# The second stream of the RWKV mixer runs 37 of its 74 stages behind the first, on every engine

## The reference

```python
def step(s, inp):
    r_t, w_t, k_t, v_t, kk_t, a_t = inp
    sa = jnp.einsum('bhij,bhj->bhi', s, -kk_t)
    s = (s * w_t[:, :, None, :] + sa[..., None] * (kk_t * a_t)[:, :, None, :]
         + v_t[..., None] * k_t[:, :, None, :])
    return s, jnp.einsum('bhij,bhj->bhi', s, r_t)
...
y = ((y - mean) * lax.rsqrt(var + GN_EPS) * p['rwkv_ln_w'][j].reshape(H_B, N_B)
     + p['rwkv_ln_b'][j].reshape(H_B, N_B))
y = y + jnp.sum(r * kb * p['rwkv_r_k'][j], axis=-1, keepdims=True) * v
o_b = y.reshape(bsz, T, D_B) * gate
```

## Time and profile before

| | |
|---|---|
| median of three runs | 3694.82 us (3686.28 to 3708.57) |
| span of the profiled execution | 3677.0 us |
| PE busy | 3407.4 us, 93% |
| DVE, ACT, POOL busy | 46%, 32%, 45% |
| mean granted clock of TensorE | 0.947 |
| RWKV mixer within the span | about 603.0 to 921.5 us |

### The profile page before, as it was taken

The page is one execution under the profiler, slowest core; times in us unless marked ns, Lnnn a source line. Parts: engine busy times, 40 slices in busy tenths (PEclk is TensorE's granted clock), DMA queues, the critical chain, the costliest instruction groups (busy, mean ns, idle before and its releaser), DMA issues.

```text
span 3677.0 us, 63816 instructions
## 1 busy us (share of the span) xinstructions
PE 3407.4 (93%) x24784; PEld 3270.7 (89%) x24784; DVE 1678.0 (46%) x2251; ACT 1169.2 (32%) x1384; POOL 1643.6 (45%) x1038
## 2 busy tenths in 40 slices
PE   7998896857879999999999799998979999999997
PEld 7998885846879999999999699985979999999997
DVE  3236667485563332233334546814563332233345
ACT  3244443231333332233322235421233332233322
POOL 4556773000444444544444455721444445444443
PEclk9999997978889999999999899986989999999999
DMA  5443331000424444444443444542424444444442
GB/s 166 151 150 111 122 105 55 4 24 15 153 88 149 148 150 159 137 149 148 148 159 133 148 145 124 173 144 120 145 91 148 148 155 154 137 149 148 155 150 107
DMA packets 118658, 474.81 MB, mean 129 GB/s; under 512 B 13425, under 2 KB 15089, under 8 KB 115569
## 3 DMA queue, kind: packets, MB, share of 16 engines
q1 hardware_dynamic: 108864, 421.58, 35.8%
q10 hardware_dynamic: 9648, 51.17, 3.6%
HBM read 450.66 MB, written 22.03 MB: 129 GB/s over the span
## 4 chain that ended last, share of the span: by engine, by line
PE 86%; DVE 9%; ACT 2%; issue 1%; POOL 1%; DMA 1%; ACTq 0%; DVEq 0%; POOLq 0%
PE ps L316 50%; PE ps L320 25%; DVE M L462 1%; PE ps L1719 1%; PE ps L1739 1%; DVE xn L425 1%; PE ps L837 1%; PE ps L1316 1%; POOL x_lo L433 1%; PE ps L418 0%; PE ps L1318 0%; PE ps L1280 0%; DVE Z L718 0%; PE ps L1265 0%; PE ps L1482 0%
## 5 line engine op out<-in xcount | busy, mean ns | idle before, releaser
L291 POOL TENSOR_TENSOR w_lo<-raw,w_hi 128x512 fp32r<-128x512 f32 (+2 forms) x756 | 1463.6, 1937 | 1734.7 <-ACT w_hi L280 1733.9
L316 PE MATMUL ps<-x_hi,w_hi 128*128 128x320 f32 x5024 | 1515.7, 315 | 89.8 <-POOL x_lo L433 71.8
L316 PE MATMUL ps<-x_lo,w_hi 128*128 128x320 f32 x5024 | 1504.1, 313 | 0.0
L280 ACT ACTIVATE w_hi<-raw 128x1024 fp32r<-128x1024 f32 (+1 forms) x756 | 840.8, 1113 | 1654.3 <-PE ps L320 1618.2
L316 PEld LDWEIGHTS ps<-x_hi,w_hi 128*128 128x128 f32 x5024 | 959.8, 191 | 107.9 <-issue 73.6
L291 DVE TENSOR_TENSOR w_lo<-raw,w_hi 128x512 fp32r<-128x512 f32 (+1 forms) x640 | 515.8, 807 | 1030.0 <-ACT w_hi L280 1012.1
L316 PEld LDWEIGHTS ps<-x_lo,w_hi 128*128 128x128 f32 x5024 | 961.8, 191 | 0.6
L320 PE MATMUL ps<-x_hi,w_lo 128*128 128x320 f32 x5024 | 846.4, 311 | 1.9 <-POOL w_lo L291 1.9
L320 PEld LDWEIGHTS ps<-x_hi,w_lo 128*128 128x128 f32 x5024 | 769.5, 189 | 2.9 <-POOL w_lo L291 2.9
L316 PE MATMUL ps<-u_hi,w_hi 128*128 128x320 f32 x1408 | 415.5, 310 | 6.3 <-DVE u_lo L530 6.3
L316 PE MATMUL ps<-u_lo,w_hi 128*128 128x320 f32 x1408 | 415.1, 309 | 0.0
(11 more groups left out here) (359 smaller groups left out, 2606.9 us busy)
## 6 DMA issues: line engine op xcount, KB each, us to landing
raw<-in_w_ffn_in SPq DMA_DIRECT2D x352, 512.0 KB, 3.5
raw<-in_w_ffn_out SPq DMA_DIRECT2D x128, 704.0 KB, 4.0
raw<-in_w_in_even SPq DMA_DIRECT2D x116, 512.0 KB, 3.5
raw<-in_w_in_odd SPq DMA_DIRECT2D x96, 512.0 KB, 3.5
raw<-in_w_out_even SPq DMA_DIRECT2D x32, 512.0 KB, 3.5
raw<-in_w_out_odd SPq DMA_DIRECT2D x32, 512.0 KB, 3.5
hS<-in_state_hgrn ACTq DMA_DIRECT2D x4, 1024.0 KB, 5.5
out_hgrn_s<-hS ACTq DMA_DIRECT2D x4, 1024.0 KB, 4.9
```

What stands on the lines that cost most here:

```text
L280: nc.scalar.activation(w_hi[s % 2][:, 0:g.kt, :], raw[s % 4][:, 0:g.kt, :], ACT.Copy)\
L291: eng.tensor_tensor(w_lo[s % 2][:, k0:k1, :], raw[s % 4][:, k0:k1, :], w_hi[s % 2][:, k0:k1, :].bitcast(f32), sub).then_inc(sem(f"split_lo ...
L316: nc.tensor.matmul(out, w_hi[s % 2][:, k, :], x[:, kk, :], start=half == 0 and k == 0 and x is xh, stop=False)
```

## The change

Stream 1 gets the stage numbers of its groups raised by ROFF = 37. On every engine the instructions are the same ones as before; only how the two streams are merged changes. Stream 0 passes through its first 37 stages alone, stream 1 through its last 37 alone; between them one stream's stages 37 to 73 stand beside the other's stages 0 to 36, three times. Waits on semaphores, buffers and banks are unchanged.

```diff
-        RJ, RGROUPS, RSTAGES = 2, 4, 74
+        RJ, RGROUPS, RSTAGES, ROFF = 2, 4, 74, 37
...
# rwkv_act, rwkv_dve and rwkv_pe:
-                j0, at0 = RJ * g, G * RSTAGES
+                j0, at0 = RJ * g, G * RSTAGES + ROFF * x
...
# rwkv_pool:
-                yield G * RSTAGES + 6
+                yield G * RSTAGES + ROFF * x + 6
```

## The result

| | before | after |
|---|---|---|
| time, median | 3701.7 us (4 runs, 3686.3 to 3710.4) | 3770.8 us (4 runs, 3761.9 to 3776.7) |
| ratio | | 1.020, 95% interval 1.017 to 1.024 |
| span of the profiled execution | 3677.0 us | 3774.8 us |
| RWKV mixer in it (last L799 to L296) | 318.5 us | 393.3 us |

The change makes the kernel 2% slower, and the mixer accounts for it. VectorE does the same work. TensorE's busy time has grown by 66 us though its instructions are the same. ScalarE (ACT) has seven instructions more, 1391 for 1384: all of them are loads of an activation table, which the text of the kernel does not contain. In the mixer these loads went from 9 to 16, at 1.28 us each. Two streams in like stages shared one load for each kind of function; now almost every group needs its own. What they cost is told behind the experiments.

A forecast was written before the change was run, and what follows sets the result against it. No engine was taken as full over the whole 318.5 us mixer; each piece has its own limit. 72.9 + 247.6 + 6 + 46.0 = 372.5, 54 more, so 3694.8 + 54 = 3749 us, range 3720 to 3780.

The forecast's parts named there:

- A1: Mixer start, one stream alone in stages 0 to 36 (set-up, transposes, Gram blocks, doubling): 72.9 us.
- M: One mix, a stream's stages 37 to 73 beside the other's 0 to 36: 81.5, 84.6 and 81.5 us.
- B1: Mixer end, one stream alone in stages 37 to 73 (five chunks, states, group norm): 46.0 us.
- rival 4: Lone stream's doubling runs at the low clock: 13 us more in A1, some 6 in B1, 3768 us; chance 0.17.
- Rival 3: Queues serialize the mixes more, M about 93 us: mixer 79 us more, 3774 us; chance 0.16.
- the signs: In the mixer: first L1093 steps about 68, 84, 87 us, last some 133 before L296, TensorE busy share near 0.6.
- The three mixes: Middle of the mixer, walked through the queues: 81.5 + 84.6 + 81.5 = 247.6 us, before 6 for the clock.
- The 6 us at the last block: End of a mix: VectorE's 7.5 us reciprocal block stands before the other stream's last XT, 6 us more.
- The clock in the mixes: Doubling level 2 behind the narrow S products runs at the low clock: about 2 us a mix, 6 in all.
- Table loads: ScalarE's activation table loads were to stay the same number, nothing added or removed.
- Rivals 1 and 2: Mixes: first, chains share well, M 65 to 72.7, chance 0.09; second, busiest engine alone binds, M 55.6, 3662 us, chance 0.03.
- The time around the mixer: Outside the mixer: the 17.8 us between profiled span 3677.0 and median 3694.8 taken as unchanged.

The follow-up runs named there:

- e_tail: Changed kernel with VectorE's reciprocal block of the tail one and a half stages later, behind the other stream's last XT; ratio to before 1.021, mixer 397.9 us.
- e_s0wide: Changed kernel with a group's 32 S products of 16 columns replaced by 4 of 128 columns, first sequence's state alone; ratio to before 1.017, mixer 383.9 us.
- e_phase80: Changed kernel with RSTAGES = 80 and ROFF = 40, the ending group three stages further ahead in each mix; ratio to before 1.025, mixer 409.0 us.
- e_warm: Changed kernel with products added whose result nobody reads, only where a stream is alone; ratio to before 1.020, mixer 381.1 us.
- e_bwarm: Kernel before, no offset, with 48 unread products behind L1249 and 16 behind stream 1's Gram blocks; ratio to before 0.999, mixer 317.6 us.

## Why the prediction was right, and what in it was not

The forecast was +54 us and 3749 us; the mixer came out 74.9 longer, the time 69 by the medians and 75 by the ratio, inside the range of 3720 to 3780. The sign and its reason (A1 + 3M + B1, with lone parts that no partner covers) held. The size was 21 us short: 3770.8 lies outside the 3728 to 3762 that had the chance of 0.55, and next to rival 4's 3768, which had 0.17; the range held it because it was drawn around rivals 3 and 4 too. Of the signs, the first L1093 follow at 74.4, 83.7 and 89.3 (68, 84, 87 forecast), the last stands 136.6 before L296 (133), and TensorE's busy share is 0.67 (0.6). Of rival 4's sign, levels of 8 us and more, two of the lone levels met it (8.84 and 8.08) and two did not.

- **The three mixes**: forecast 81.5, 84.6 and 81.5 with 6 for the clock, 253.6 in all; measured 83.7, 89.3, 84.7, 257.7. In the first mix the walk was off by less than 2 us at each mark: L1120 ended 21.1 us in (20.7 forecast), the last L1074 30.5 (29.3), XI 42.8 (41.9), level 4 73.4 (71.6). The 6 us at the last block were 4.6, but e_tail showed that they are no fault of the order: either group waits for the other there.
- **The clock in the mixes**: 6 us were forecast, 2 behind the S products in each mix. About 6 came out, but by luck. Behind the S products the clock fell in the second mix alone: level 2 took 2.79 (L1308) and 3.27 (L1316) there, and 1.58 and 2.48 in the other two, at a clock of 1.00; e_s0wide brings the second mix to 1.33 and 2.48. That is 2.0 us. What was at the low level in all three mixes is the first level, which the sum took "at full clock" there: 2.40 instead of 1.38 for L1308 and 2.8 instead of 2.48 behind it, 1.3 us a mix, 4.0 in all. The first two rows are levels 1 and 2 of the first mix, the last two those of the second:

```profile
730.30:732.70 2.40, 2.40 (x43) 2.40 (x44) 0.00 (x0) 0.00 (x0) 0.00 (x0) 0.50 0.03 7
740.90:745.60 4.70, 4.31 (x142) 4.17 (x140) 0.69 (x1) 1.32 (x4) 0.00 (x0) 1.00 0.02 3
813.50:815.90 2.40, 2.40 (x46) 2.40 (x48) 0.00 (x0) 0.00 (x0) 0.00 (x0) 0.50 0.02 7
826.30:832.50 6.20, 6.20 (x132) 6.01 (x132) 0.69 (x1) 1.43 (x4) 0.00 (x0) 0.61 0.01 3
```

- **Table loads**: "Nothing is added or removed; table loads of ScalarE stay the same number" was wrong. Seven more loads are 9.0 us of ScalarE. By the rows they hardly reach the path: in the mixes, eleven of the twelve loads ended 0.03 to 2.6 us before their function could start, since it waited for another engine. The twelfth is the root of the second mix, whose variance (L1393) had ended at 850.42, 0.7 us before the load:

```profile
849.18 0.60 ACT L1035 ACTIVATE T<-ps 128x512 f32<-128x512 f32 x1 [1.76 <-PE ps L1308]
849.80 1.28 ACT L1065 ACT_TABLE_LOAD   x1
851.09 0.94 ACT L1065 ACTIVATE ySQ<-ps,com 128x320 f32<-128x320 f32 x2
```

No experiment took the loads away, so what they delay in the ending stream's chunks is not shown.

- **A1**: forecast 72.9, measured 78.8. This is the term that failed by mechanism. The doubling was costed "from rows at full clock" plus 3 us for a slow first level; it ran at 0.66. XT came 8.84, 8.08, 6.85 and 5.35 us apart. With the clock kept high they are 6.69, 5.94, 5.54 and 4.64, near the 6.8, 5.5, 5.5 and 4.0 of the sum, and A1 is 69.8. The set-up part of the sum held: the last of XT and XI ended 41.3 us in, 41.2 forecast.
- **B1**: forecast 46.0, measured 56.9, the largest miss. A chunk was 6.81, not 4.9; at the high level it is 5.34, so 1.5 of it is the clock and 0.4 the step. S products were put at 3.4 and took 5.80, at the high level 3.28. From the last L1172 to L296 26.4 was forecast, 31.9 measured, 29.4 at the high level. So 5.4 us of the miss of 10.9 are shown to be the clock (twice 1.47 in the chunks, 2.5 in the tail), and 6.9 if the third interval of the chunks is priced like the two. That the rest is round trips of the tail, halved in the forecast from a tail with two streams, is argued and was not tried.
- **Rival 4** (the lone stream at the low level) was thus not an alternative to the forecast but a part of it: its 13 + 6 us were 9.0 in A1 and, by the chunks and the tail above, 5.4 to 6.9 in B1. It belonged into the sum, since the earlier trace rows already had a first level at the low clock behind an idle stretch.
- **Rivals 1 and 2**: steps of 83.7 and 89.3 rule out 65. In this case interleaving a VectorE stretch with a TensorE stretch made the work of two groups 172 us long instead of 159. The Trainium skill, Perfetto Trace Analysis, section Optimization Strategy, says that interleaving such regimes may improve performance; in this case's trace it did not.
- **Rival 3** (M of 93): 86 measured on average, between the forecast's 84.5 (its clock term included) and this; only e_phase80 came near, with steps of 89 to 91.
- **The time around the mixer** was taken as "unchanged", with 17.8 us between span and time. Time and span of the same execution differ by under 2 us (3776.65 and 3774.8 in after). So the 17.8 were scatter from execution to execution. The profiled execution of before had the shortest retention part of all (92.7), and the stretch ahead of the mixer scatters too (it ended between 603.1 and 608.7).

## What to carry to other kernels

Two streams in the same phase look wasteful where one engine is full at a time, but before offsetting them price the start and the end: an offset of half a group left 136 us of lone chain to win back, and the mixes won nothing. Count also what two like streams share, such as the loads of activation tables. Walk the chain of each stream through the queues; where both end in the same block of an in-order engine, reordering only chooses who waits. And price lone stretches at the clock that a lone stream gets, not at that of rows where another stream filled the gaps.

## What the runs showed of the hardware

TensorE's granted clock was 0.50 in 950 to 970 of after, where TensorE was busy for 79% and idle for 0.4 to 0.8 us at a time between small products. Products whose result nobody reads, put into those gaps, went with a clock of 1.00 (650 to 677 of e_warm) and 0.94 (941 to 960). They did not always do: in 963 to 970 of e_warm the clock was 0.54 with TensorE busy for all of the 7 us. Nor did narrow products always bring it down: with the S products (16 columns) it stayed at 1.00 in the first and third mix of after and fell in the second.

An idle time of 4.3 us behind 12 us in which TensorE was busy all the time was followed by ten transposes at 2.34 instead of 1.25 us, at a clock of 0.50 (e_bwarm, 638 to 641). In retention the low level, once there, stayed through two blocks of 512 columns of 7.19 us each in some executions (2532 to 2553 of after: clock 0.50, TensorE busy for 21.0 of 21 us), and in others the clock was back before them (3.95 and 3.88 in before): 93, 104 or 117 us for the same instructions.

A load of an activation table took 1.28 us of ScalarE. Sixteen stood in the mixer of after and nine in that of before, since there two streams in like stages share a load.
